# A blocked triangular inverse on the tensor engine: 64 moving columns a matmul in place of 128

## What is computed

```python
a_mat = jnp.where(strict, jnp.einsum('bhncd,bhnsd->bhncs', kb, k) * gamma, 0.0)
eye = jnp.eye(C, dtype=q.dtype)
t_mat = lax.linalg.triangular_solve(eye + a_mat, jnp.broadcast_to(eye, a_mat.shape),
                                    left_side=True, lower=True, unit_diagonal=True)
```

```python
sa = jnp.einsum('bhij,bhj->bhi', S, a_t)
S = S * w_t[:, :, None, :] + sa[..., None] * b_t[:, :, None, :] + v_t[..., None] * k_t[:, :, None, :]
y = jnp.einsum('bhij,bhj->bhi', S, r_t)
```

## Time and profile before

| | |
|---|---|
| median of 3 runs | 3457.5 us (3450.93 to 3460.96) |
| profiled execution, span | 3455.0 us |
| TensorE busy | 3102.8 us, 90% |
| weight loads busy | 3013.8 us, 87% |
| VectorE busy | 2019.1 us, 58% |
| ScalarE busy | 1403.6 us, 41% |
| GpSimd busy | 203.3 us, 6% |

### The profile page before, as it was taken

One profiled execution on the slowest core, in us unless ns is written; L12 is line 12 of the kernel. 1 busy time (PEld: TensorE's weight loads), 2 busy tenths in 40 slices (PEclk: granted clock), 3 DMA queues, 4 the chain that ended last, 5 costly groups with the idle time before them and its releaser, 6 DMA issues.

```text
span 3455.0 us, 56680 instructions
## 1 busy us (share of the span) xinstructions
PE 3102.8 (90%) x24296; PEld 3013.8 (87%) x24296; DVE 2019.1 (58%) x2219; ACT 1403.6 (41%) x1710; POOL 203.3 (6%) x128
## 2 busy tenths in 40 slices
PE   7987678989899999999986997788689999999986
PEld 7886677989899999999986986677589999999986
DVE  5466645455556766676676555555465555555554
ACT  4355323233444444444453443322244444444442
POOL 1010011000010000000001001100010000000010
PEclk9998889999999999999998998899799999999998
DMA  6633323345455565656552641000046555655543
GB/s 199 176 110 110 86 85 92 92 141 165 150 171 169 184 185 173 189 171 191 179 172 86 183 121 49 25 25 31 7 144 194 179 182 178 194 182 185 182 137 110
DMA packets 251820, 482.14 MB, mean 140 GB/s; under 512 B 16784, under 2 KB 22032, under 8 KB 251440
## 3 DMA queue, kind: packets, MB, share of 16 engines
q1 hardware_dynamic: 251568, 478.52, 45.3%
HBM read 476.36 MB, written 2.10 MB: 138 GB/s over the span
## 4 chain that ended last, share of the span: by engine, by line
PE 66%; DVE 17%; ACT 8%; DMA 4%; issue 3%; POOL 1%; DVEq 0%; POOLq 0%; ACTq 0%; SPq 0%
PE psm L327 55%; PE psb L382 10%; DVE slo L269 5%; ACT ar L395 3%; DVE ar L398 3%; DVE ar L406 3%; ACT shi L267 2%; DMA raw<-in_w_up 1%; DMA raw<-in_w_down 1%; ACT gh L395 1%; DVE gf L398 1%; DVE ar L409 1%; DVE x L398 1%; POOL ar L398 1%; DMA raw<-in_w_ple_gate 1%
## 5 line engine op out<-in xcount | busy, mean ns | idle before, releaser
L269 DVE TENSOR_TENSOR slo<-raw,shi 128x1024 fp32r<-128x1024 f32 (+1 forms) x901 | 1141.4, 1275 | 816.9 <-ACT shi L267 810.1
L267 ACT ACTIVATE shi<-raw 128x1024 fp32r<-128x1024 f32 (+1 forms) x901 | 936.3, 1051 | 1150.0 <-PE psm L327 772.1
L327 PE MATMUL psm<-gh,shi 128*128 128x256 f32 x4544 | 1324.1, 291 | 41.3 <-DVE slo L269 32.8
L327 PE MATMUL psm<-gl,shi 128*128 128x256 f32 x4544 | 1299.7, 286 | 0.0
L327 PE MATMUL psm<-gh,slo 128*128 128x256 f32 x4544 | 1298.8, 286 | 0.0
L327 PEld LDWEIGHTS psm<-gh,shi 128*128 128x128 f32 x4544 | 885.0, 195 | 51.5 <-DVE slo L269 35.4
L327 PEld LDWEIGHTS psm<-gl,shi 128*128 128x128 f32 x4544 | 884.5, 195 | 6.3 <-issue 4.7
L327 PEld LDWEIGHTS psm<-gh,slo 128*128 128x128 f32 x4544 | 883.2, 194 | 0.5
L327 PE MATMUL psm<-hh,shi 128*128 128x256 f32 x2528 | 734.4, 290 | 51.9 <-DVE hl L414 20.4
L327 PE MATMUL psm<-hl,shi 128*128 128x256 f32 x2528 | 724.4, 287 | 0.0
L327 PE MATMUL psm<-hh,slo 128*128 128x256 f32 x2528 | 723.8, 286 | 0.0
(11 more groups left out here) (185 smaller groups left out, 1487.0 us busy)
## 6 DMA issues: line engine op xcount, KB each, us to landing
raw<-in_w_in SPq DMA_DIRECT2D x240, 512.0 KB, 3.7
raw<-in_w_up SPq DMA_DIRECT2D x176, 512.0 KB, 4.3
raw<-in_w_ffn_up SPq DMA_DIRECT2D x128, 512.0 KB, 3.8
raw<-in_w_ffn_down SPq DMA_DIRECT2D x128, 512.0 KB, 3.8
raw<-in_w_down SPq DMA_DIRECT2D x88, 512.0 KB, 4.2
raw<-in_w_out SPq DMA_DIRECT2D x64, 512.0 KB, 3.7
raw<-in_w_ple_gate SPq DMA_DIRECT2D x32, 512.0 KB, 4.1
raw<-in_w_branch_b SPq DMA_DIRECT2D x16, 512.0 KB, 3.7
```

The lines of the kernel that those rows point to most:

```text
L267: th = A.do(lambda e: e.activation(shi[:, s, 0:m], raw[:, q, 0:m], ACT.Copy), landed, pe_tok.get(j - NS), chain=False)
L269: lo_tok[j] = V.do(lambda e: e.tensor_tensor(slo[:, s, 0:m], raw[:, q, 0:m], shi[:, s, 0:m].bitcast(F), ALU.subtract), landed, th, chain=F ...
L327: e.matmul(out, l, r, start=st, stop=sp, skip_group_check=True),
```

## The change

The matmuls get only the half of the columns that can change as moving operand: X's first columns of each pair for M X, Y's first columns for P, XT's second columns for Q. So four matmuls write 256 columns of a bank, packed, where they wrote 512. The mask `lv` is stored packed as well, 64 columns a level. The mask multiply reads the packed 256 elements and writes every other block of Y. Y's other columns are never written after a memset of Y to zero, which GpSimd does at the start of each inversion, between XT's second operation and the point where VectorE makes X's identity; that VectorE operation now waits for the memset. At later levels Y also holds stale columns of earlier levels. In Q they show up as rows, and the update of XT multiplies Q by a column of 0 and -1 (`hm`) before it adds, in one scalar_tensor_tensor on VectorE. The number of matmuls is the same.

```diff
--- before.py
+++ after.py
@@ -33,7 +33,7 @@
 CON = {}
 _at = 0
 for _n, _k in (("ident", 128), ("ones", 128), ("bones", 128), ("perm", 128), ("utri", 256),
-               ("lv", 6 * 128), ("nm0", 128), ("nm0t", 128), ("cm", 128), ("reset", 256),
+               ("lv", 6 * 64), ("hm", 6), ("nm0", 128), ("nm0t", 128), ("cm", 128), ("reset", 256),
                ("rcnt", 64), ("invf", 1)):
     CON[_n] = (_at, _k)
     _at += _k
@@ -65,7 +65,9 @@
         b = 1 << n
         same = (i[:, None] // (2 * b)) == (i[None, :] // (2 * b))
         lv.append((same & ((i[:, None] // b) % 2 == 1) & ((i[None, :] // b) % 2 == 0)).astype(np.float32))
-    put("lv", np.concatenate(lv[1:], 1))
+    low = [i[(i // (1 << n)) % 2 == 0] for n in range(7)]
+    put("lv", np.concatenate([lv[n][:, low[n]] for n in range(1, 7)], 1))
+    put("hm", np.stack([-((i // (1 << n)) % 2 == 0).astype(np.float32) for n in range(1, 7)], 1))
     put("nm0", -lv[0])
     put("nm0t", -lv[0].T)
     cm = np.where(i[None, :] > i[:, None], np.float32(-1e30), np.float32(0))
@@ -565,40 +567,53 @@
                 m4 = b.ap.rearrange("p (a b) -> p a b", a=4)
                 tp = trs([(m4[:, m, :], mt[:, m, :]) for m in range(4)], t_mt, *b.free)
                 tt(XT, mt, bc(C("nm0t"), 4), ALU.mult, t_mt, *inv_free, q=P)
-                tq = P.do(lambda e: e.tensor_tensor(XT, XT, bc(C("ident"), 4), ALU.add))
+                P.do(lambda e: e.tensor_tensor(XT, XT, bc(C("ident"), 4), ALU.add))
+                tq = P.do(lambda e: e.memset(Y, 0.0))
                 yield
                 tv = tt(X, m4, bc(C("nm0"), 4), ALU.mult, tp, *inv_free)
                 b.free = (tv,)
-                tv = tt(X, X, bc(C("ident"), 4), ALU.add)
+                t_X = t_XT = tt(X, X, bc(C("ident"), 4), ALU.add, tq)
                 for l in range(6):
                     s = 2 << l
+
+                    def half(ap, low):
+
+                        return ap.rearrange("p (g h s) -> p g h s", h=2, s=s)[:, :, low, :]
+
+                    def halves(ap, low):
+                        return ap.rearrange("p a (g h s) -> p (a g) h s", h=2, s=s)[:, :, low, :]
+
+                    def packed(bk):
+
+                        return bk.ap[:, 0:256].rearrange("p (g s) -> p g s", s=s)
+
+                    def mat(bk, m):
+                        return bk.ap[:, 64 * m:64 * m + 64].rearrange("p (g s) -> p g s", s=s)
+
                     b = bank()
-                    y4 = b.ap.rearrange("p (a b) -> p a b", a=4)
-                    tp = mms([(y4[:, m, :], mt[:, m, :], X[:, m, :], m == 0, True) for m in range(4)],
-                             tv, tq, *b.free)
-                    tv = tt(Y, y4, bc(C("lv", 128 * l, 128), 4), ALU.mult, tp)
-                    b.free = (tv,)
+                    tp = mms([(mat(b, m), mt[:, m, :], half(X[:, m, :], 0), m == 0, True) for m in range(4)],
+                             t_X, t_XT, *b.free)
+                    lv = C("lv", 64 * l, 64)
+                    lv = C("lv", 64 * l, 64).rearrange("p (g s) -> p g s", s=s).unsqueeze(1)
+                    t_Y = tt(Y.rearrange("p a (g h s) -> p a g h s", h=2, s=s)[:, :, :, 0, :],
+                             b.ap[:, 0:256].rearrange("p (a g s) -> p a g s", a=4, s=s),
+                             lv.to_broadcast([128, 4, 64 // s, s]), ALU.mult, tp)
+                    b.free = (t_Y,)
                     yield
-
-                    def half(ap, low):
-                        return ap.rearrange("p a (g h s) -> p (a g) h s", h=2, s=s)[:, :, low, :]
-
                     if l < 5:
                         b = bank()
-                        p4 = b.ap.rearrange("p (a b) -> p a b", a=4)
-                        tp = mms([(p4[:, m, :], XT[:, m, :], Y[:, m, :], m == 0, True) for m in range(4)],
-                                 tv, *b.free)
+                        tp = mms([(mat(b, m), XT[:, m, :], half(Y[:, m, :], 0), m == 0, True) for m in range(4)],
+                                 t_Y, *b.free)
                     b2 = bank()
-                    q4 = b2.ap.rearrange("p (a b) -> p a b", a=4)
-                    tp2 = mms([(q4[:, m, :], Y[:, m, :], XT[:, m, :], m == 0, True) for m in range(4)],
-                              tv, *b2.free)
+                    tp2 = mms([(mat(b2, m), Y[:, m, :], half(XT[:, m, :], 1), m == 0, True) for m in range(4)],
+                              t_Y, *b2.free)
                     if l < 5:
-                        tv1 = tt(half(X, 0), half(X, 0), half(p4, 0), ALU.subtract, tp)
-                        b.free = (tv1,)
-                    tv = tt(half(XT, 1), half(XT, 1), half(q4, 1), ALU.subtract, tp2)
-                    b2.free = (tv,)
+                        t_X = tt(halves(X, 0), halves(X, 0), packed(b), ALU.subtract, tp)
+                        b.free = (t_X,)
+                    t_XT = stt(halves(XT, 1), packed(b2), C("hm", l, 1), halves(XT, 1), ALU.mult, ALU.add, tp2)
+                    b2.free = (t_XT,)
                     yield
-                self.tok = tv
+                self.tok = t_XT
 
 
         V.wait(t_par)
```

## The result

The changed kernel takes 3493.6 us (median of 4, 3486.7 to 3502.7) against 3455.4 us of the kernel before, run beside it: a ratio of 1.0112, 95% interval 1.0093 to 1.0132. It is 38 us slower. The profiled execution has a span of 3484.9 us, 29.9 more than the profiled one of before, with the same 24296 matmul records. At 3486.7 us it is the fastest of the four, 7 us under their median; its trace shows the loss at its smallest.

The account below looks back on a forecast made before the run. TensorE was taken as the bound, 90% busy, with the inversion's own chain counting too in the second place. 3455.0 - 15 + 12 + 63 = 3515 us, forecast 3517 with the runs' median 2.5 above the span; range 3440 to 3580 us.

Parts of the forecast that it names:

- The load sets the pace: Inversion matmuls: weight loads, not moving columns, set the pace; 0.107 in place of 0.111 us a record, 6.5 us less.
- Group tails: Last matmul of a group, not pipelined, 0.05 us shorter at each of TensorE's 42 waits: 2.2 us less.
- Mask multiply 0.42 us: VectorE's mask multiply falls from 0.692 to about 0.424 us, counting at 26 of 42 waits: 7.0 us less.
- Memset 0.5 us, hidden but once: GpSimd's memset of Y, awaited by VectorE, costs time only in the last inversion: 0.6 us, at most 1.4.
- Last inversion at 1.2 GHz: Last inversion, running alone: levels 2 to 5 at 7.16 in place of 4.53 us, last level 1.6 more; together 12 us.
- First place without a price: First four inversions, 477 to 566 and 621 to 705 us: big products between all steps, unchanged within 3 us.
- PEclk in slices 25 to 29 at 7 or lower: Sign expected: TensorE's clock, in tenths, at 7 or lower in these time slices, which hold the dense stretches.
- Dense stretches, half of 126 us: Second place's 2140-2198, 2245-2307, 2357-2416 us, 1264 records: 0 to 126 us more at 1.2 GHz; middle taken, 63.
- Rival 1: TensorE's clock stays up in the dense stretches and only the 15 us gain is left: 3442 us; chance 0.16.
- Rival 2: Dense stretches hold the clock nearly always, only the last inversion goes cold: 3455 to 3460 us; chance 0.07.
- rival 3: Inversion matmuls take time by their columns, 1632 records x 0.055 us = 90 us: 3385 us; chance 0.03.
- rival 4: Dense stretches all cold at 1.2 GHz: 3580 us, the far end of the forecast's mechanism, which had 0.74 in all.

Follow-up runs that it names:

- e11: Changed kernel plus unread matmuls in the last group alone: four ahead of G, four ahead of the inversion, two ahead of mask and XT x Y products; 3478.1 us.
- e10: Changed kernel with 128 moving columns in the last inversion of the second place, 64 everywhere else; 3485.3 us.
- e6: Changed kernel with 128 moving columns in the products XT x Y and Y x XT, only the mask product at 64; 3466.4 us.
- e1: Changed kernel with the matmuls' moving columns back at 128, the rest of the change kept; 3448.7 us, ratio 0.9977 to the kernel before.
- e9: Changed kernel with 128 moving columns everywhere except in the last inversion of the second place, which has 64; 3466.1 us.
- e3: Changed kernel with 64 moving columns only in the first block's four inversions, 128 in the second block's eight; 3453.6 us.
- e4: Changed kernel with 64 moving columns only in the second block's eight inversions, 128 in the first block's four; 3492.6 us.
- e2: Kernel before with only the three products' moving operands and outputs halved to 64 columns, in place; 3493.6 us, ratio 1.0104.
- e7: e1 plus unread matmuls in each group of the second place, ahead of G, the inversion and the last sum; 3453.3 us.
- e8: Changed kernel plus one unread matmul ahead of each mask product and each XT x Y, in the last inversion alone; 3499.0 us.

## Why the prediction was right, and by how much it was off

The sign and the cause were right and the time lies in the range, but that range, 3440 to 3580 us, also holds a small gain and no change. The size was off: 3517 us was 60 above the median then at hand, and 38 came. Its largest term, 63 us, was the middle between two ends, and no row decided between them; that the forecast came no further off is partly luck, since errors of both signs met. By the steps:

- **The load sets the pace:** right. 16 loads take 1.86 and 3.49 us as before, so a record of 64 columns costs what one of 128 does. The term of 0.004 us a record (6.5 us) was mis-sized: (1.86 - 0.19)/15 is still 0.111 us, so it is nothing. It was read off 16-column matmuls at 1.2 GHz and carried over to 64 columns, where no difference is seen at either clock. Short runs of moving columns cost nothing, as said: in e11 the 16 records take 1.89 to 1.90 us at each of the first five levels.
- **Group tails:** right. At 1.2 GHz 16 records take 3.68 us, against 3.78 with 128 columns (e10); at 2.4 GHz 8 records take 1.08 us (e6) against 1.13 (e1), the 0.05 us of the prediction.
- **Mask multiply 0.42 us:** right (425 ns). **XT's update at nothing:** wrong, 484 ns against 421; I had read a row without a column of scalars, and the row with one said 485. **Memset 0.5 us, hidden but once:** right, 526 ns. VectorE's one wait was 1.2 us, and TensorE's idle time ahead of the last inversion grew from 2.12 us to 2.71, the 0.6 us that I had. Together I had 7.0 - 0.6 = 6.4 us of gain for these, and e1 has 8.7.
- **Last inversion at 1.2 GHz:** right, levels of 6.80 us for "near 6.7", clock 0.50 for 65 us. Taken 12 us; the traces part by 17 there. Levels 2 to 5 give 9.1 of it and the last level 1.8, near my 12. What I left out are the products behind the inversion, 4.3 us more up to the next big product, and those ahead of it, 1.1: they had 2.4 GHz before and have 1.2 now. By medians e9 gives 19.5 against e1.
- **First place without a price:** wrong, 5 us (e3), outside my "unchanged within 3 us". Big products between the steps did not hold the clock everywhere.
- **PEclk in slices 25 to 29 at 7 or lower:** so in three of the five; two have 8.
- **Dense stretches, half of 126 us:** the term that was mis-sized most. For my 63 us the traces of this program show 12 to 29 against the kernel before, and the medians some 24 against e1 (43.9 of e4 less 19.5 of e9). Two things failed. The share: over the same work (the three windows above) a clock of 0.88, 0.78 and 0.75 is 64, 122 and 147 us at 1.2 GHz. The 58 and 83 us more hold at most 276 and 395 records at 0.21 us each, 28 and 40 us at 0.100 more a record; I had taken half of 1264, 632 records. And the price: TensorE's busy time grew by 21 and 35 us, and 9 and 6 of these came out of its idle time, so that 12 and 29 appeared. That a slower TensorE fills waits for VectorE which existed anyway is how I read the shrinking idle time; no run tested it by itself.

Put together by medians, against e1: 5.0 in the first place (e3), 24 in the dense stretches, 19.5 in the last part, less the 8.7 that e1 gains: 40 us, for the 38 found; each of these differences is uncertain by some 5 us. I had 0, 63, 12 and 15. The dense term was 39 too high; the last part 7.5 too low, the first place 5 too low and the gain 6.3 too high, and these three made up for half of it. Rival 1 (the clock stays up) did not come; e1, where the columns are whole, shows 3448.7 us. Rival 2 fails at the dense stretches, rival 3 at the loads, rival 4 at the same place, where 1.2 GHz holds for 44 and 50% of the time (122 of 277 and 147 of 294 us).

**Open:** why e2, without VectorE's savings, is no slower than the changed kernel (36.2 us above before against 38.3), when those savings are worth 8.7 us with full columns. In the last inversion they do show, a level of 6.94 us in e2 and 6.80 in the changed kernel; elsewhere the spread of the dense stretches, 12 to 29 us from trace to trace, is larger than what is looked for.

## What to carry to other kernels

Before you halve the columns of a matmul whose weights are loaded anew each time, see whether the loads set its pace; if they do, as here, there is nothing to gain and the clock to lose. Where TensorE works alone and thinly, read the granted clock of the stretch first: a few unread matmuls in its waits can be worth more than the work saved, and the same ones are a loss where TensorE is already the bound (e7). A cost per slow instruction is an upper bound wherever the engine also waits: charge the stretch, not the record. And where executions of one program differ, as the dense stretches did, size a part from several traces over the same work.

## What the runs showed of the hardware

- A TensorE without any idle time for 32.6 us ran at 1.2 GHz throughout (e8), and one that was busy 14 of 20 us had 0.98. Between 64 and 128 moving columns, at the same pace of records and both entered at 1.2 GHz, lies the difference between never regaining 2.4 GHz (e9) and regaining it after one level (e10).
- A clock that has risen can fall again during the same pattern of work: with the 107 columns of e6 the first level was at 1.2 GHz, the second at 2.4, and within the third it fell to 1.2 for the rest.
- A scalar_tensor_tensor of 256 f32 elements with a column of scalars from SBUF took 484 ns, one without it 424; a GpSimd memset of 512 f32 elements took 526 ns.
- The same 1511 matmul records took 276.9, 287.0, 294.1 and 294.1 us in four traces of one program (changed kernel, e8, e10, e11). Whole executions of the changed kernel spread over 16 us; those of the kernel before spread over 10 (4 of them) and 14 (21 of them, beside e1 to e4).
